# Hybrid trunk kernel on one core: order of the loads between the up and the down projection

## What is computed

```python
h = rms_norm(x, norm1_g)
u, q, k, v = split(h @ w_in)
a = pool_mixer(u, pool_w, pool_scale)
b = swa_sink_attention(q, k, v, q_norm_g, k_norm_g, sinks)
x = x + concat(a, b) @ w_out            # the kernel's x1
h2 = rms_norm(x, norm2_g)
hid = square(relu(h2 @ w_up))           # 1024 x 4096
x = x + hid @ w_down
```

## Time and profile before

| | us |
|---|---|
| median of 3 runs | 915.49 |
| the three runs | 915.1, 915.49, 917.33 |
| the profiled execution, its own time | 917.33 |
| its span, first to last instruction | 915.5 |
| PE busy in it | 889.9 (97%) |
| DVE busy | 558.4 (61%) |
| ACT busy | 422.5 (46%) |
| POOL busy | 281.2 (31%) |

### The profile page before, as it was taken

How to read it: one execution, slowest core, us unless ns; L and a number is a source line. 1 busy time by engine, 2 the same in 40 slices (tenths; PEclk the granted TensorE clock), 3 DMA queues, 4 the chain that set the end, 5 groups by cost and what they waited for, 6 DMA issues and landing times.

```text
span 915.5 us, 11013 instructions
## 1 busy us (share of the span) xinstructions
PE 889.9 (97%) x4161; PEld 737.3 (81%) x4161; DVE 558.4 (61%) x797; ACT 422.5 (46%) x762; POOL 281.2 (31%) x197
## 2 busy tenths in 40 slices
PE   6999999999999689999999999999999999999998
PEld 5888888778888468888888888877888888888886
DVE  6566666864437977666766667554965454656462
ACT  6466666742212455556555565443433334333340
POOL 1443333600006233322443224201544103444440
PEclk9999999999999889999999999999999999999999
DMA  8100101535112055543554335389952462252522
GB/s 310 47 24 24 71 24 47 162 115 161 47 46 70 1 177 167 162 127 127 173 173 160 127 127 177 129 314 392 339 187 97 152 235 92 70 161 69 184 78 84
DMA packets 65724, 124.19 MB, mean 136 GB/s; under 512 B 3580, under 2 KB 20488, under 8 KB 65672
## 3 DMA queue, kind: packets, MB, share of 16 engines
q1 hardware_dynamic: 65648, 123.49, 39.8%
q10 hardware_dynamic: 24, 0.01, 0.0%
HBM read 85.73 MB, written 37.75 MB: 135 GB/s over the span
## 4 chain that ended last, share of the span: by engine, by line
PE 84%; DVE 8%; DMA 3%; ACT 2%; issue 2%; POOL 1%; SPq 0%; DVEq 0%; ACTq 0%
PE bank L1266 26%; PE bank L1267 26%; PE bank L1268 26%; DVE t_tmp L1047 2%; DVE h_buf L1078 2%; PE bank L1285 1%; PE bank L1386 1%; PE bank L1398 1%; DMA d_raw<-in_w_down 1%; DMA s_in<-h_keep 1%; PE bank L1374 1%; POOL mem L467 1%; DMA h_keep<-h_buf 1%; PE bank L1366 1%; DVE wgt L922 0%
## 5 line engine op out<-in xcount | busy, mean ns | idle before, releaser
L1266 PE MATMUL bank<-b_op,s_op 128*128 128x512 f32 x448 | 175.2, 391 | 2.5 <-DVE b_op L1089 2.5
L1268 PE MATMUL bank<-b_op,s_op 128*128 128x512 f32 x448 | 175.0, 391 | 0.0
L1267 PE MATMUL bank<-b_op,s_op 128*128 128x512 f32 x448 | 174.8, 390 | 0.0
L542 POOL TENSOR_TENSOR b_sum<-d_raw,d_raw 128x1024 f32<-128x1024 f32 x40 | 97.6, 2439 | 204.1 <-DVE b_op L1089 204.1
L1085 DVE TENSOR_TENSOR s_op<-s_in,s_op 128x1024 fp32r<-128x1024 f32 x56 | 76.6, 1367 | 127.5 <-ACT s_op L774 127.5
L774 ACT ACTIVATE s_op<-s_in 128x1024 fp32r<-128x1024 f32 x56 | 59.4, 1060 | 181.9 <-PE bank L1268 145.7
L1029 DVE TENSOR_TENSOR ring<-raw,ring 128x512 fp32r<-128x512 f32 x92 | 86.7, 959 | 81.3 <-ACT ring L704 79.6
L1266 PE MATMUL bank<-wgt,xs 128*128 128x256 f32 (+1 forms) x320 | 124.2, 388 | 2.7 <-DVE wgt L910 2.7
L1267 PE MATMUL bank<-wgt,xs 128*128 128x256 f32 (+1 forms) x320 | 119.3, 373 | 0.0
L1268 PE MATMUL bank<-wgt,xs 128*128 128x256 f32 (+1 forms) x320 | 119.1, 372 | 0.0
L1266 PE MATMUL bank<-xs,ring 128*128 128x512 f32 x232 | 92.4, 398 | 11.5 <-DVE ring L1029 11.5
(11 more groups left out here) (125 smaller groups left out, 1390.6 us busy)
## 6 DMA issues: line engine op xcount, KB each, us to landing
s_in<-h_keep SPq DMA_DIRECT2D x56, 512.0 KB, 3.7
h_keep<-h_buf SPq DMA_DIRECT2D x16, 1280.0 KB, 5.1
raw<-in_w_up SPq DMA_DIRECT2D x16, 1024.0 KB, 6.4
d_raw<-in_w_down SPq DMA_DIRECT2D x16, 1024.0 KB, 9.1
mem<-in_x SPq DMA_DIRECT2D x16, 512.0 KB, 4.2
h_keep<-h_buf SPq DMA_DIRECT2D x16, 512.0 KB, 3.9
mem<-in_w_in SPq DMA_DIRECT2D x8, 640.0 KB, 6.6
x_keep<-mem SPq DMA_DIRECT2D x8, 512.0 KB, 2.8
```

The lines of the kernel that those rows point to most:

```text
L542: nc.gpsimd.tensor_tensor(out=b_sum[G % 2], in0=group_rows(qa, g), in1=group_rows(qb, g), op=op).then_inc(b_summed, 1)
L1266: nc.tensor.matmul(out_ap, lhs[HI], rhs[HI], start=first, stop=False, skip_group_check=chained)
L1267: nc.tensor.matmul(out_ap, lhs[HI], rhs[LO], start=False, stop=False, skip_group_check=chained)
L1268: return nc.tensor.matmul(out_ap, lhs[LO], rhs[HI], start=False, stop=last, skip_group_check=chained)
```

## The change

SP's order is changed at two places, and ACT's and DVE's at one. First, at the head of chunk 15 the first two quarters of B11 are issued ahead of `load_s(0)` to `load_s(2)`. Second, the eight loads of x1 no longer stand one by one in the down loop but all together ahead of `load_s(3)`, on one semaphore; the quarters of B22 move up by two groups. Third, the operands of group 0 are made behind product i = 3 of chunk 15 and not behind i = 4. DVE's list has the same two changed lines as ACT's in the diff, with `operands_low` for `split_operands`. DVE waits once for x1, at group 10, and no more a second time at group 26.

```diff
             for c in range(NCK):
                 if c == NCK - 1:
-                    for G in range(3):
-                        load_s(G)
                     sp.wait_ge(up_done, nth(c, 1) + 1)
                     for quarter in range(2):
                         load_d("B11", quarter)
+                    for G in range(3):
+                        load_s(G)
                     sp.wait_ge(up_done, nth(c, 3) + 1)
...
             sp.wait_ge(up_done, N_UP)
             sp.wait_ge(dve_read, 3 * (NCK - PLAIN))
+            for t in range(NT):
+                sp.dma_start(resid[t], x1_keep[t]).then_inc(x1_back, 16)
             for G in range(3, 7 * NG):
                 load_s(G)
                 if 3 <= G < 7:
                     load_d("B12", G - 3)
-                if 5 <= G < 9:
-                    bring_x1(KH + G - 5)
-                if 10 <= G < 14:
-                    load_d("B22", G - 10)
-                if 15 <= G < 19:
-                    bring_x1(G - 15)
+                if 8 <= G < 12:
+                    load_d("B22", G - 8)
...
-                    if c == NCK - 1 and i in (4, 5):
-                        split_operands(i - 4)
+                    if c == NCK - 1 and i in (3, 5):
+                        split_operands((i - 3) // 2)
...
-                    if p in (1, 3) and g == 0:
-                        dve.wait_ge(x1_back[1 if p == 1 else 0], 16 * KH)
+                    if p == 1 and g == 0:
+                        dve.wait_ge(x1_back, 16 * NT)
```

More of the change, by code:

```diff
@@ L186, in hybrid_trunk @@
         s_in_landed = [sem(f"s_in_landed{i}") for i in range(3)]
-        x1_back = [sem(f"x1_back{i}") for i in range(2)]
+        x1_back = sem("x1_back")
         zeroed, setup_pool, setup_dve, setup_done = sem("zeroed"), sem("setup_pool"), sem("setup_dve"), sem("setup_done")
@@ L321, in load_d @@
                 sp.dma_start(d_raw[q][:, js, :], w_down_i[i][:, js, k * BANK:(k + 1) * BANK]).then_inc(d_in[q][quarter], 16)
-            def bring_x1(t):
-                sp.dma_start(resid[t], x1_keep[t]).then_inc(x1_back[t // KH], 16)
             def store_out(i, k):
@@ L1246, in _ @@
                         h_add(c, DD, A11, A22, ALU.add, 3)
-                    if c == NCK - 1 and i in (4, 5):
-                        operands_low(i - 4)
+                    if c == NCK - 1 and i in (3, 5):
+                        operands_low((i - 3) // 2)
             h_add(NCK - 1, SA, A21, A22, ALU.add, 4)
```

## The result

The changed kernel is slower, by about the forecast amount (13.8 us at the median, 14.9 were forecast):

| | before | changed |
|---|---|---|
| median of 4 runs, us | 915.56 | 929.37 |
| lowest to highest, us | 915.1 to 917.33 | 929.04 to 931.38 |
| ratio, 95% interval | | 1.0152 [1.0133, 1.0172] |
| span of the profiled execution, us | 915.5 | 927.6 |

The account below looks back on a forecast made before the run. PE-bound except from 600 to 620, where PE waits for B11's first quarter and `load_s(3)`. Group 3's delay of 13.3 us plus 1.6 us of clock gave 14.9 us, on the 915.49 median 930.4 us; range 925.5 to 934.5.

Parts of the forecast that it names:

- Which loads are the gates: Up-to-down step: B11's first quarter ends PE's 1.88 us stop before group 0, `load_s(3)` the 0.64 us one before group 3.
- The queue: SP's loads drain in issue order at about 392 GB/s; group 0's left operand lands at 601.8, where B11 did.
- Rival A: Ahead of group 3: transfers pass one another, so x1 does not delay `load_s(3)`; loss 2.6 to 3.8 us, 918.7; chance 0.05.
- rival D: Ahead of group 3: x1 drains slower than 392 GB/s; at 303 GB/s 933.5, with 2.85 us of clock 934.8; chance 0.11.
- The step that took the row's rate: x1's drain priced at the trace's 392 GB/s, 10.7 us, not the skill page's 358 GB/s, 11.7 us.
- M3: Matmuls of chunk 15 waiting for `add_z(15, 1)`, now behind group 0's low parts: PE stands still about 5.7 us.
- Rival B: Chunk 15: no stop before M3, store not late, x1 still ahead of group 3; 927.8, up to 3 us less; chance 0.09.
- Store of chunk 15: Second store of chunk 15 issued at 615.0 instead of 612.51, 2.5 us later, landing at 621.3.
- Group 3: Down projection: group 3 starts at 637.0, 13.3 us later: 2.5 from the later store, 10.7 from x1.
- Clock: Behind the idle stretch ahead of group 3, PE runs at granted clock 0.50, costing 1.6 us.
- What was called free: Behind group 3: loads catch up; B22 two groups earlier, x1's wait at group 10 and its removed second wait change nothing.
- rival C: Group 0's operands ready early and x1 passing aside: group 3 at about 620.7, gain 3 us, 912.5; chance 0.03.

Follow-up runs that it names:

- first half of the repair: Kernel before, with only group 0's left operand ahead of B11's first quarter and those of groups 1 and 2 behind it: 917.58 us, ratio 1.001.
- B11 first: Kernel before, with two quarters of B11 issued ahead of the three left operands at the head of chunk 15, nothing else: 916.36 us, ratio 1.0005.

## Why the prediction was right

**Which loads are the gates.** The prediction read from the earlier trace rows that the first quarter of B11 and the left operand of group 3 were the loads that PE's two stops hang on, and foretold that group 0's left operand would take the place of B11. It held: the chain after goes through the landings of both left operands.

**The queue.** One after the other in the order of issue. Group 0's left operand landed at 590.74 + 8.76 + 1.8 = 601.3, foretold 601.8, and x1's eight tiles landed in the order of issue, the first 6.8 us after its own issue and the last 10.2 us after its own (time to landing of the eight):

```profile
L398 SPq DMA_DIRECT2D mem<-x_keep x8: 443/484/1247, 613.0 to 618.6; - x8
...
DMA to landing us min/median/max: 6.8/7.5/10.2
```

The last tile, issued at 618.6, landed at 628.8, and the store of chunk 15 had landed at 618.6: the eight tiles take 10.2 us, 411 GB/s; foretold were 10.7 at 392. Rival A, that transfers pass one another, falls with it: group 3's operand, issued behind the block, landed behind it too, 1.4 us after the last tile. So does the main part of rival D, which took 303 GB/s.

The Trainium skill ("DMA: Bandwidth & Descriptors", Specifications) gives a limit of about 358 GB/s of device memory per core; the trace is 15% above it. By that figure x1 would take an estimated 11.7 us, 1.5 us more than measured. The step that took the row's rate was the right one.

One thing the prediction did not say: most of the delay does not show as time to landing. That of group 3's left operand rose from 7.1 to 11.0 us only. The other 8 us are a later issue (619.19 + 1.8 against 613.05): 1.85 from the store, and 6.1 in which SP was issuing x1:

```profile
612.54 0.37 SPq L303 DMA_DIRECT2D h_keep<-h_buf  x1
613.00 6.08 SPq L398 DMA_DIRECT2D mem<-x_keep  x8
619.19 0.38 SPq L315 DMA_DIRECT2D s_in<-h_keep  x1
```

SP's issuing is not what set the pace: the tiles landed one every 1.3 us, the last of them 10 us after SP had begun to issue it, and while they moved (window) the DMA engines were fully busy:

```profile
618.60:628.80 10.20, 6.18 (x28) 4.78 (x26) 0.00 (x0) 0.00 (x0) 0.00 (x0) 0.95 1.03 414
```

**M3.** Foretold a stop of about 5.7 us, ended by `add_z(15, 1)`; measured 5.22, since the landing came 0.5 us sooner. That the old stop ahead of group 0 would go, and that the delay would be absorbed by the wait behind it, held too: alone it costs 2.3 us at the median, on top of x1's block 1.4. Rival B, no stop ahead of M3, falls with the 5.22 us.

**Store of chunk 15.** Foretold 2.5 us later, measured 612.54 + 1.82 - 612.51 = 1.85. Again 0.5 of the difference is the landing of the operand.

**Group 3.** Foretold 13.3 us later, measured 11.9: 1.85 from the store and 10.2 from x1, less 0.2. Both terms were a little large, in the same direction.

**Clock.** Foretold 1.6 us, measured 2.2: after 9 us of idle PE it ran 4.3 us at the lower of its two levels, 1.2 GHz, where the row chosen as nearest had 3.0 us. This term was too small and gives back part of the 1.4 us above: 11.9 + 2.2 = 14.0 against 14.9. That the errors of the terms had opposite signs was luck; the mechanism does not hang on it.

**What was called free** was free: from 638 to 895 PE is busy for all of the 257 us, with B22 and the x1 wait in their new places. And rival C, faster, would have needed the left operand before 597.6; it landed 3.7 us later. A slip in the prediction: the low end of rival B, up to 3 us under 927.8, is 924.8 and lies outside the range that is said to take B in.

The median moved by 13.8 us, the profiled spans by 12.1, and the sum had been made on a profiled execution that stood 1.8 us above the median. The prediction carried the difference over to the median without asking where the 1.8 us were from. That was right: the two traces side by side show that they belong to the front half of that execution.

## What to carry to other kernels

When loads share one queue, price a moved load by the bytes that now stand ahead of the next load that someone waits for: 4 MB cost nothing in one place and 10 us in the other, a few lines apart. A load of an operand can go ahead of a store that is not ready yet, if its buffer is free and what it reads was stored long before, as here; that alone took 11 us from the changed kernel. Between two gates in a row a gain at the first is only worth what the second lets through: open the later gate first, or both.

## What the runs showed of the hardware

A stop of PE need not be long for the clock to fall behind it. Behind stops of 1.88 us (before), 2.27 us (first half of the repair) and 2.46 us (B11 first) it ran some 3.4 us at 1.2 GHz; behind stops of 0.67 and 0.33 us it stayed at 2.4 GHz. The window of the second stop is above (622.50 to 626.00: 0.51); those of the first and the third:

```profile
605.50:608.90 3.40, 3.40 (x10) 2.63 (x9) 1.79 (x2) 3.37 (x5) 0.00 (x0) 0.50 1.04 378
```

```profile
603.50:606.80 3.30, 3.30 (x8) 2.62 (x9) 1.12 (x1) 3.27 (x5) 0.00 (x0) 0.50 0.96 348
```

A repair that shortens a stop from 1.9 to 0.7 us can thus gain more than the 1.2 us. A wait that is pushed to a later place can take its half clock along, as the first half of the repair shows.

Tiles with rows of 4 KB came in a little faster than those with 2 KB, 10.2 us for 4.19 MB (411 GB/s, or 414 in the window above) against the 385 to 395 GB/s of the windows in which mostly 2 KB rows moved. That the row length is the cause was not tested; the tiles of x1 also come from another place in device memory.
